# A hybrid encoder layer on one core: first loads in pieces, sums spread, six packed transposes per attention block

## The reference

```python
xn = rmsnorm(x, g_mix)
u_lru, y_lru, q, k, v, gates = jnp.split(xn @ w_in, IN_SPLITS, axis=-1)
xc, lru_conv_new = causal_dwconv(u_lru, lru_conv_prev, w_lconv, b_lconv)
h, lru_h_new = rg_lru(xc, lru_h_prev, w_a, b_a, w_i, b_i, lam)
br_lru = (h * jax.nn.gelu(y_lru)) @ w_br_lru
q = rmsnorm(q.reshape(B, T, N_HEADS, HEAD_DIM), g_q)
k = rmsnorm(k.reshape(B, T, N_KV_HEADS, HEAD_DIM), g_k)
br_attn = attn_fn(q, k, v, sink) @ w_br_attn
x = x + (g[:, :, 0] * br_lru + g[:, :, 1] * br_attn) @ w_out
gate_pre, up = jnp.split(rmsnorm(x, g_ffn) @ w_up, [D_FF], axis=-1)
gc, ffn_conv_new = causal_dwconv(gate_pre, ffn_conv_prev, w_fconv, b_fconv)
x = x + (jax.nn.gelu(gc) * up) @ w_down
```

## Time and profile before

| | us |
|---|---|
| three runs | 1802.4, 1808.53, 1806.59 |
| median | 1806.59 |
| profiled execution, its own time | 1809.89 |
| its span, first to last instruction | 1808.1 |
| PE busy, share of the span | 99% |
| DVE, ACT, POOL busy | 46%, 31%, 28% |
| mean granted clock of PE | 0.992 |

### The profile page before, as it was taken

The page is one execution under the profiler, slowest core; times in us unless marked ns, Lnnn a source line. Parts: engine busy times, 40 slices in busy tenths (PEclk is TensorE's granted clock), DMA queues, the critical chain, the costliest instruction groups (busy, mean ns, idle before and its releaser), DMA issues.

```text
span 1808.1 us, 29895 instructions
## 1 busy us (share of the span) xinstructions
PE 1794.6 (99%) x11252; PEld 1746.7 (97%) x11252; DVE 838.0 (46%) x1624; ACT 561.4 (31%) x1117; POOL 499.8 (28%) x282
## 2 busy tenths in 40 slices
PE   9999999999999999999999999999999999999999
PEld 8998888899999999999999999999999999999999
DVE  7946757711247676112465555411555511555511
ACT  5535544400156765112133332200322300333300
POOL 3112101122332232333332333332223333333222
PEclk9989989999999999999999999999999999999999
DMA  4011000011111111111311111111111111111113
GB/s 162 25 30 42 24 24 24 24 50 46 39 47 41 52 38 38 47 46 46 143 47 36 46 46 46 47 46 47 46 46 42 41 46 46 46 46 46 46 46 121
DMA packets 28514, 89.16 MB, mean 49 GB/s; under 512 B 3472, under 2 KB 8496, under 8 KB 28464
## 3 DMA queue, kind: packets, MB, share of 16 engines
q1 hardware_dynamic: 25200, 82.49, 13.7%
q10 hardware_dynamic: 3264, 5.96, 1.0%
HBM read 83.70 MB, written 4.73 MB: 49 GB/s over the span
## 4 chain that ended last, share of the span: by engine, by line
PE 95%; DVE 2%; ACT 2%; issue 0%; DMA 0%; SPq 0%; ACTq 0%; DVEq 0%
PE banks L440 85%; PE banks L560 2%; PE banks L575 2%; PE banks L516 1%; PE banks L549 1%; PE banks L526 1%; PE banks L716 1%; PE banks L715 1%; DVE x_lo L1198 1%; DMA resid<-xT 0%; DVE x_lo L1183 0%; DVE resid L1191 0%; ACT prB L910 0%; DVE merged L1206 0%; DVE prB L1298 0%
## 5 line engine op out<-in xcount | busy, mean ns | idle before, releaser
L440 PE MATMUL banks<-x_hi,w_hi 128*128 128x352 f32 x1752 | 578.5, 330 | 4.6 <-DVE x_lo L1183 3.1
L440 PE MATMUL banks<-x_hi,w_lo 128*128 128x352 f32 x1752 | 568.5, 324 | 0.0
L440 PE MATMUL banks<-x_lo,w_hi 128*128 128x352 f32 x1752 | 566.8, 324 | 0.0
L409 POOL TENSOR_SCALAR w_hi<-w_raw 128x1024 fp32r<-128x1024 f32 x137 | 157.0, 1146 | 1238.4 <-DMA w_raw<-W 1238.4
L440 PE MATMUL banks<-h_hi,w_lo 128*128 128x352 f32 x1152 | 372.7, 323 | 0.0
L440 PE MATMUL banks<-h_hi,w_hi 128*128 128x352 f32 x1152 | 372.4, 323 | 0.0
L440 PE MATMUL banks<-h_lo,w_hi 128*128 128x352 f32 x1152 | 371.6, 323 | 0.0
L440 PEld LDWEIGHTS banks<-x_hi,w_hi 128*128 128x128 f32 x1752 | 331.6, 189 | 9.0 <-issue 3.1
L411 POOL TENSOR_TENSOR w_lo<-w_raw,w_hi 128x1024 fp32r<-128x1024 f32 x137 | 334.1, 2439 | 11.4
L440 PEld LDWEIGHTS banks<-x_lo,w_hi 128*128 128x128 f32 x1752 | 331.1, 189 | 2.9
L440 PEld LDWEIGHTS banks<-x_hi,w_lo 128*128 128x128 f32 x1752 | 330.5, 189 | 0.0
(11 more groups left out here) (212 smaller groups left out, 1819.7 us busy)
## 6 DMA issues: line engine op xcount, KB each, us to landing
w_raw<-W SPq DMA_DIRECT2D x139, 512.0 KB, 3.4
resid<-xT SPq DMA_DIRECT2D x6, 704.0 KB, 9.8
sqsum<-xT ACTq DMA_DIRECT2D x2, 2112.0 KB, 13.4
o_yT<-resid SPq DMA_DIRECT2D x8, 528.0 KB, 4.6
wabs<-wab ACTq DMA_DIRECT2D x8, 128.0 KB, 2.0
w_early<-W SPq DMA_DIRECT2D x1, 512.0 KB, 3.7
mat<-mats SPq DMA_DIRECT2D x1, 192.0 KB, 10.1
vec<-vecs SPq DMA_DIRECT2D x1, 143.0 KB, 2.3
```

Source lines behind the costliest of these rows:

```text
L409: nc.gpsimd.tensor_scalar(w_hi[s][:, :], w_raw[s][:, :], 1.0, 0.0, ALU.mult, ALU.add).then_inc(w_hi_done, 1)
L440: last = nc.tensor.matmul(out[:, 0:cn], w[s if wt is None else wt][:, k * P:(k + 1) * P], x[:, k, cc:cc + cn], start=(k == 0 and j == 0), ...
```

## The change

What the first two loads and their splits work on is halved or quartered: SP loads the first weight in two halves, x's first chunk in four pairs of rows, the second weight in two halves; ACT loads vec. ACT copies both weights' w_hi by halves and does the squares of chunk 0 behind them; DVE makes both w_lo by halves; POOL splits neither. PE waits for halves (w_first, then wx_ready or wy_ready at k = 4). Warm-up has four matmuls instead of six.

Key sums move to later k steps (the last into the V halves). The query sums of group 0 are spread over 24 k steps of six V halves, one or two units ahead of each three V matmuls; those of group 1 over 15 k steps of the fills of blocks 12, 13 and 14, two or three units each, from the third step of a fill on.

Probabilities of a block lie packed: 4 x 192 columns, in pr0 or pr1. For b = 2 to 15 (28 blocks) PE transposes 2 x 384 columns in 6 transposes: head 0's first 128 keys, head 0's last 64 with head 1's first 64, head 1's last 128. So each head has a full product and one of 64 keys, which take the lower 64 partitions of pt for head 0 and the upper 64 for head 1. Their V chunks must lie on the same partitions, so ACT copies V shifted by one chunk into vsh by DMA, four DMAs for each group (`shift_v`). The products run as full, full, half, half.

ACT copies V tile 6 out ahead of exps(0). The last LRU gates move to k steps (0, 2), (0, 6) and (1, 2), and the first tile that needs the last LRU row runs k = 0 to 6 of all three chunks before k = 7 of any. The last row of y is stored in three pieces. The main lines (definitions and renames are left out):

```diff
@@ -364,14 +366,19 @@

         @block.sync
         def _(sp):
-            sp.dma_start(vec[:, :], vecs).then_inc(s_vec, 16)
-            sp.dma_start(w_raw[0][:, :], W[0]).then_inc(wx_loaded, 16)
-            for n, (c0, cn) in enumerate(CHUNKS):
+            left, right = slice(0, DM // 2), slice(DM // 2, DM)
+            sp.dma_start(w_raw[0][:, left], W[0][:, left]).then_inc(s_half[0], 16)
+            for r in range(KT // 2):
+                kk, (c0, cn) = slice(2 * r, 2 * r + 2), CHUNKS[0]
+                sp.dma_start(resid[:, kk, c0:c0 + cn], xT[kk, :, c0:c0 + cn].rearrange("k p n -> p k n")).then_inc(s_x0[r], 16)
+                if r == 0:
+                    sp.dma_start(w_raw[0][:, right], W[0][:, right]).then_inc(wx_loaded, 16)
+            sp.dma_start(w_raw[1][:, left], W[1][:, left]).then_inc(s_half[1], 16)
+            sp.dma_start(w_raw[1][:, right], W[1][:, right]).then_inc(wy_loaded, 16)
+            for n, (c0, cn) in list(enumerate(CHUNKS))[1:]:
                 for h in range(2):
                     kk = slice(h * KT // 2, (h + 1) * KT // 2)
                     sp.dma_start(resid[:, kk, c0:c0 + cn], xT[kk, :, c0:c0 + cn].rearrange("k p n -> p k n")).then_inc(s_x[2 * n + h], 16)
-                    if (n, h) == (0, 0):
-                        sp.dma_start(w_raw[1][:, :], W[1]).then_inc(wy_loaded, 16)
             sp.dma_start(mat[:, :, :], mats).then_inc(s_mat, 16)
             sp.wait_ge(x_done, 1)
             sp.dma_start(early[:, :], W[4]).then_inc(s_early, 16)
...
+                sp.dma_start(yT[KT - 1, :, c0:c0 + cn], resid[:, KT - 1, c0:c0 + cn]).then_inc(s_out, 16)
+            sp.wait_ge(s_out, 16 * (6 + 3 + KT + 2))


         @block.gpsimd
...
             pool.wait_ge(s_early, 16)
             pool.wait_ge(x_rlo, 3 * KT)
             nc.gpsimd.tensor_scalar(w_hi[2][:, :], early[:, :], 1.0, 0.0, ALU.mult, ALU.add).then_inc(s_ehi, 1)
...

                 def before(k):
+                    if n == 0 and k == 0:
+                        pe.wait_ge(w_first, s + 1)
+                    elif n == 0 and k == KT // 2:
+                        pe.wait_ge(wx_ready if s == 0 else wy_ready, 1)
...
-            for _ in range(6):
+            for _ in range(4):
...
-            def v_half(tt, s):
+            def v_half(tt, s, sums=None):

                 t0 = tt * P if tt < SEQ // P else T - P
                 to = bank[tt % 6]
                 for k in range(4 * s, 4 * s + 4):
+                    if sums is not None:
+                        query_sums(0, sums + k - 4 * s, SUMS_STEPS)
                     for j, (w, x) in enumerate(((w_hi, x_hi), (w_hi, x_lo), (w_lo, x_hi))):
...
+            def query_sums(a, step, steps):
+
+                for i in range(step * UNITS // steps, (step + 1) * UNITS // steps):
+                    t0 = SMP if i == UNITS - 1 else i * DSEQ
...
-                for i, (c0, kn, _) in enumerate(groups_of(b)):
-                    for v in range(2 * units_of(b)):
-                        last = nc.tensor.transpose(bank[6 + i][0:kn, v * P:v * P + P], pr_of(b)[:, v, c0:c0 + kn], ident)
...
+                else:
+                    for i, to in enumerate((0, 4, 2)):
+                        for u in range(2):
+                            out = bankpair[3].rearrange("p b n -> p (b n)")[:, (to + u) * P:(to + u + 1) * P]
+                            last = nc.tensor.transpose(out, pr_of(g, 0, u, i * P, P), ident)
...
+                elif b > 1:
+                    pe.wait_ge(s_vsh, 64 * (a + 1))
                 n = units_of(b) * P
-                for e in range(2):
-                    ch = slice(a * P + 64 * e, a * P + 64 * e + 64)
-                    for i, (_, kn, m) in enumerate(groups):
-                        v = vcs[0:kn, ch] if m is None else vtok[0:kn, m, ch]
-                        last = nc.tensor.matmul(bank[3][64 * e:64 * e + 64, 0:n], v, pt[0:kn, i, e * n:e * n + n],
-                                                start=(i == 0), stop=(i == len(groups) - 1))
+
+                def times(e, v, rows, c0, first, last_):
+                    return nc.tensor.matmul(bank[3][64 * e:64 * e + 64, 0:n], v[rows, :], pt[rows, c0:c0 + n], start=first, stop=last_)
+
...
+                else:
+                    for e, two in ((0, b - 2), (1, b - 1)):
+                        times(e, vtok[:, two // 2, heads[e]] if two % 2 == 0 else shifted(e, two), every, e * 2 * P, True, False)
+                    for e, one in ((0, b), (1, b - 2)):
+                        last = times(e, vtok[:, one // 2, heads[e]] if one % 2 == e else shifted(e, one), (lower, upper)[e], 4 * P, False, True)
...
+                def before(k):
+                    nonlocal at
+                    if at == SUMS_FROM:
+                        pe.wait_ge(a_lo, g)
+                        if g == SUMS_BLOCKS[0]:
+                            pe.wait_ge(x_act, out_before(PAIR_G))
+                            pe.wait_ge(y_act, out_before(PAIR_G))
+                    if at >= SUMS_FROM:
+                        query_sums(1, first + at - SUMS_FROM, steps * len(SUMS_BLOCKS))
+                    at += 1
+                for (s, p, n), ks in fill_of(g):
+                    beside(s, p, n, ks, before)
...
-                elif (n, k) == (1, 0):
+                elif (n, k) == (1, 4):
                     key_sum(0, 2)
+                elif (n, k) == (2, 0):
                     key_sum(1, 0)
-                elif (n, k) == (2, 0):
+                elif (n, k) == (2, 4):
                     key_sum(1, 1)
...
                 v_half(tt, 0)
+                if tt == 1:
+                    key_sum(1, 2)
             pe.wait_ge(wy_ready, PAIR_V + 1)
+            pe.wait_ge(h_sqd, 12)
+            pe.wait_ge(h_rt, 5)
             for tt in range(3):
-                v_half(tt, 1).then_inc(v_done, 1)
+                v_half(tt, 1, 4 * tt).then_inc(v_done, 1)
             pe.wait_ge(h_rt, 6)
             for tt in range(6, 9):
                 pe.wait_ge(v_free, tt - 5)
-                v_half(tt, 0).then_inc(x_done, 1)
-                if tt == 6:
-                    pe.wait_ge(h_sqd, 12)
-                for b in SUMS_AT[tt - 6 + NB - 4]:
-                    query_sums(0, b)
+                v_half(tt, 0, 4 * (tt - 3)).then_inc(x_done, 1)
             for tt in range(3, 6):
                 v_half(tt, 1).then_inc(v_done, 1)
             v_half(6, 1).then_inc(y_done, 1)
...
-            def gated(p0, stage, between=None, second=None, before=None):
+            def last_gates(n, k):
+
+                if (n, k) == (0, 2):
+                    pe.wait_ge(s_wab, 16 * KT)
+                    lru_gates(KT - 1, 0)
+                elif (n, k) in ((0, 6), (1, 2)):
+                    lru_gates(KT - 1, n + 1)
...
+                pe.wait_ge(wx_ready, p0 + 2)
+                for n in range(3):
+                    chunk(0, n, c_hi, d_lo, ks=range(KT - 1))
+                for n in range(3):
+                    chunk(0, n, c_hi, d_lo, last_row(r_lo, START + 3 * (KT - 1), n), ks=range(KT - 1, KT))
...
+            act.dma_start(vec[:, :], vecs).then_inc(s_vec, 16)
...
+            left, right = slice(0, DM // 2), slice(DM // 2, DM)
+            act.wait_ge(s_half[0], 16)
+            A(w_hi[0][:, left], w_raw[0][:, left], ACT.Copy).then_inc(s_w0, 1)
             act.wait_ge(s_vec, 16)
-            for h in range(2):
-                unscaled_hi(0, h)
-                squares(0, (h,))
+            for r in range(KT // 2):
+                c0, cn = CHUNKS[0]
+                act.wait_ge(s_x0[r], 16)
+                for k in (2 * r, 2 * r + 1):
+                    A(x_hi[:, k, c0:c0 + cn], resid[:, k, c0:c0 + cn], ACT.Copy, scale=V("g_mix", k)).then_inc(x_rhi, 1)
+                if r == 1:
+                    act.wait_ge(wx_loaded, 16)
+                    A(w_hi[0][:, right], w_raw[0][:, right], ACT.Copy).then_inc(s_w0, 1)
+            act.wait_ge(s_half[1], 16)
+            A(w_hi[1][:, left], w_raw[1][:, left], ACT.Copy).then_inc(s_w1, 1)
+            act.wait_ge(wy_loaded, 16)
+            A(w_hi[1][:, right], w_raw[1][:, right], ACT.Copy).then_inc(s_w1, 1)
+            squares(0)
...
             query_root(0)
+            v_out(6)
             act.wait_ge(h_rdy, 6)
             exps(0)
-            for tt in range(6, 9):
+            for tt in range(7, 9):
                 v_out(tt)
...
+            def shift_v(a):
+
+                n = NC // 2
+                for e, (low, up) in enumerate(((slice(0, n), slice(0, n - 1)), (slice(1, n), slice(0, n)))):
+                    ch = slice(a * P + 64 * e, a * P + 64 * e + 64)
+                    act.dma_start(vsh[0:CHUNK, low, e, :], vtok[CHUNK:P, 0:low.stop - low.start, ch]).then_inc(s_vsh, 16)
+                    act.dma_start(vsh[CHUNK:P, up, e, :], vtok[0:CHUNK, 1 - e:up.stop + 1 - e, ch]).then_inc(s_vsh, 16)
+
+            act.wait_ge(v_free, 9)
+            shift_v(0)
...
+                if g == NB:
+                    shift_v(1)
...
```

(35 more changed lines are left out.)

126 lines of the change are left out of this document (64 added, 62 removed).

## The result

| | before | after |
|---|---|---|
| median of the runs made together (4 each) | 1807.56 us | 1793.75 us |
| lowest and highest | 1802.40, 1810.41 | 1792.71, 1795.80 |
| profiled execution | 1809.89 (span 1808.1) | 1792.71 (span 1790.9) |
| mean granted clock over the span | 0.992 | 1.000 |

The ratio is 0.9928 (95% interval 0.9903 to 0.9953): 13.8 us or 0.7% faster, beyond the 0.3% that can be told here. The profiled executions differ by 17.2 us; the one of the changed kernel is the fastest of its four, whose spans are 1790.9, 1791.2, 1792.7 and 1794.0. Faster was forecast with 0.72, and 1793.75 is inside the range; the forecast itself, 1786.9, was 6.9 us too fast.

The account below looks back on a forecast made before the run. PE itself was taken as the bound, so gains come from fewer instructions, fewer waits or restored clock. Terms summed to 19.7 us: 1806.6 - 19.7 = 1786.9 us median (1790.2 profiled), own range 1781 to 1793, with rivals 1781 to 1809.

Parts of the forecast that it names:

- start: Beginning to norm sums: POOL's weight split no longer slows DVE's x_lo, PE arrives at 24.9, not 28.77; gain 3.8 us.
- query sums, group 0: V stage: spreading the sums among V matmuls keeps the full clock; 8.5 us back, changes cost up to 1.8; gain 6.5.
- V copy: ACT's v_out(6) goes ahead of the first exponentials and their table load, removing a PE wait; gain 1.4 us.
- small wait behind it: PE's 1.0 us wait behind the V copy, from exponentials DVE delivered late during POOL's split; gain 0.5 us.
- attention blocks: 28 blocks: six transposes for eight save 5.9 us, one more tile shape change each costs 4.5; net gain 1.4.
- query sums, group 1: Fills of three attention blocks: 5.2 us of lost clock return, 15 changes cost 1.2; gain 3.8 us.
- second shift of V and DVE's pr: Four DMAs on ACT's queue ahead of exps(18): costed at nothing, or up to 1.4 us if that block lacks slack.
- gates: Last gates: PE's 0.5 us wait for d_lo goes, 0.3 of the 0.9 for ACT's tanh stays; gain 1.1 us.
- rival (a): Attention blocks: half products run one after the other, costing 12.0 us and leaving a gain of 7.7: 1799 us; chance 0.10.
- (b): Query sums: full clock holds in only one of the two mixes, gain loses 4 to 9 us: about 1794; chance 0.12.
- (c): Query sums: clock falls in both mixes, some 5 us into the mix: about 1808 us, no change; chance 0.18.
- (d): Query sums: clock falls in each mix's first steps and rises only well behind it, making the kernel slower: 1816 us; chance 0.12.

Follow-up runs that it names:

- closed groups: Changed kernel with the queries' sums of squares back in three groups of 24, 24 and 18 records per head pair: 1801.38 us, ratio 0.9968.
- clumps: Changed kernel with the query sums in clumps of 10 to 12 records, one ahead of each V half, two per attention fill: 1792.49 us, ratio 0.9927.

## Why the prediction was right or wrong

By the profiles the sum was 19.7 us and 17.2 came. The steps, in us (the measured ones add up to 17.4 by rounding):

| step | forecast | measured |
|---|---|---|
| start | 3.8 | 1.3 |
| key sums | 0.5 | 0.3 |
| query sums, group 0 | 6.5 | 7.9 |
| V copy | 1.4 | 1.4 |
| small wait behind it | 0.5 | 0.3 |
| attention blocks | 1.4 | 2.2 |
| query sums, group 1 | 3.8 | 4.9 |
| second shift of V and DVE's pr | 0 | -1.0 |
| gates | 1.1 | -0.8 |
| last store | 0.7 | 0.9 |

That the sum is only 2.5 off is in part luck: the start, the gates, the second shift and two small terms are 5.8 too high, the query sums, the blocks and the store 3.5 too low.

**Right:** that PE is the bound and the clock the largest part of it; that the mix of three wide and a few thin matmuls holds the full level (undone and confirmed); that half products run side by side (rival (a) gone) and a change of shape costs 0.15; that ACT is what is late next at the fourth V half. Rivals (b), (c) and (d) are excluded by the clock of 1.00 in both stretches.

**The start** failed at the sentence that its gain is kept because DVE's and ACT's work starts from PE's norm products. PE got to the norm sums 2.9 us earlier (of 3.8: ACT's next group of x_hi began at 14.61, not at 13.76 as I had kept it, since ACT had waited 1.4 us for its second pair of rows of x). The work behind does start from there, but POOL's split starts from DVE's x_lo, which came only 1.1 us earlier, and the norm's small DVE operations moved up into it: 1.5 us lost by the first spread. I had the 6.96 us of the same kind in the earlier trace rows before me and asked only where the change removed such a collision, not where it makes one.

**The gates** failed at the deferred rows. I priced them as more matmuls ahead of d_lo, which came (the two waits shrank by 0.4 and 0.5, of 1.1 forecast), and not as a first chunk that ends 42 matmuls later, with ACT's table load behind it (begun at 704.08 us, with the old rows and gates at 698.43): the new wait of 1.8. The later LRU gates also brought POOL's split beside DVE's last products, 3 us that the deferred rows happen to cover.

**The second shift of V** was costed at nothing, or at up to 1.4 if the block had no slack. It had none: 1.0, with issues of 0.65 us where the row for another DMA had 0.36.

**Query sums:** the mechanism held. Their size is a matter of which execution of before is taken: 12.8 us against the profiled one, 8.9 in medians of closed groups against clumps, and 10.3 forecast.

**From the sum to the median** was the largest error, 4.4 of the 6.9 us. I carried the 3.3 us by which the profiled execution of before lay above its median over to the changed kernel. The runs' mean clocks say what that excess is: the profiled execution is like the 14 runs at 0.992, while the median was taken over three runs, one of which took 1802.4 us, as runs at 0.997 do. It goes away with the low clock: the changed kernel's profiled execution lies 1.0 below its median. The two clock terms were read from one execution of before at a low mean clock, and so hold against it and not against the median.

## What to carry to other kernels

Where PE is never idle and the clock still falls, look for stretches of matmuls of a few columns; break them up with wide ones, and clumps are as good as a fine mix. When a change makes something earlier, list what each other engine starts from: here POOL's splits met DVE's operations in new places, which took back 1.5 us at the start and would have cost 5 at the gates with the old order of rows. When work is deferred so that an operand can come late, ask also who waits for its first result. And if runs spread with the thing that the change removes, don't carry the excess of one profiled run over the median over to the changed kernel.

## What the runs showed of the hardware

- The granted clock fell to 1.2 GHz with PE busy all the time: in the kernel before 0.7 us behind its first closed group of 24 two-column records (2.6 us), with the groups put back 1.3 us behind the second of two such groups with 12 wide ones (1.5 us) between. It stayed at 2.4 GHz with clumps of 10 to 12. The low level lasted 6.8 us in one profile and 17.1 us in another for the same groups, and runs at a mean clock of 0.997 and 0.992 differ by some 7 us. It also fell behind a wait in which PE was busy 0.46 of 4.94 us. The Trainium skill ("TensorE: Matmul & The Clock Gate", Part 1: The HAM clock gate) ties the fall to an idle engine; the last case agrees with that, the first ones show it with a busy engine, and a sum that goes by the page, without a term for the clock, would leave out the 8.9 us.
- Row tiles of different rows and columns write one bank at the same time (two 64*64 products started within 0.01 us of each other), against the Trainium skill's "TensorEngine Tiling (Array Packing)", Restrictions and Gotchas, Gotcha 1: PSUM Pressure, by which different row tiles can't; the measurement decides. A change of tile shape between products (128\*64 to 64\*64) costs 0.15 us, and neighbours of unequal shape didn't run side by side even in different column halves (2.30 us for 1.16).
- A DVE operation of 0.15 us on four to six columns took 1.66 and 2.34 us beside POOL's subtraction of 2.4 us, and ended with it. The Trainium skill ("SBUF — State Buffer", SBUF: two separate sides) states that DVE, with two inputs in SBUF, and a POOL operation that reads SBUF hold a common pair of ports in turn, and that the loser is blocked for the whole of the other's operation. These rows agree with it; I had not used it to look for new collisions.
- A DMA from SBUF to SBUF in pieces of 64 channels held ACT's queue 0.63 to 0.70 us for its issue, one to memory 0.36.
